# Stick-breaking attention of a four-layer trunk: one head at a time against head pairs by key blocks

## What is computed

```
def stick_breaking_block(q, k, v, q_pos, k_pos):
    z = jnp.einsum('bqhd,bkhd->bhqk', q, k) * (SB_HEAD_DIM ** -0.5)
    mask = k_pos[None, :] < q_pos[:, None]
    log_not = jnp.where(mask, jax.nn.log_sigmoid(-z), 0.0)
    rev = lax.cumsum(log_not, axis=3, reverse=True)
    tail = jnp.pad(rev[..., 1:], ((0, 0), (0, 0), (0, 0), (0, 1)))
    a = jnp.where(mask, jnp.exp(jax.nn.log_sigmoid(z) + tail), 0.0)
    return jnp.einsum('bhqk,bkhd->bqhd', a, v)
```

## Time and profile before

| what | value |
|---|---|
| median of 3 runs | 3169.05 us (3168.03 to 3176.56) |
| the profiled execution, first to last instruction | 3168.0 us |
| TensorE, VectorE, ScalarE, GpSimd busy | 2996.5, 1217.0, 877.9, 404.1 us |
| attention of one layer, first transpose to last values | 212.1 us |
| mean granted TensorE clock, whole span / between 225.1 and 396.6 us | 0.96 / 0.92 |

### The profile page before, as it was taken

The page is one execution under the profiler, slowest core; times in us unless marked ns, Lnnn a source line. Parts: engine busy times, 40 slices in busy tenths (PEclk is TensorE's granted clock), DMA queues, the critical chain, the costliest instruction groups (busy, mean ns, idle before and its releaser), DMA issues.

```text
span 3168.0 us, 49615 instructions
## 1 busy us (share of the span) xinstructions
PE 2996.5 (95%) x20839; PEld 2804.5 (89%) x20839; DVE 1217.0 (38%) x1596; ACT 877.9 (28%) x971; POOL 404.1 (13%) x557
## 2 busy tenths in 40 slices
PE   6999999999999599999998789999999899999998
PEld 6975599999999599999997679999999655999998
DVE  3332233333433543333346554333442322433433
ACT  2124432222311232222223233222321343322222
POOL 4023310000100500000103520000000232100001
PEclk8998999999999699999999889999999999999999
DMA  3230022222222122222221012222232200222221
GB/s 125 79 113 0 1 67 80 83 85 85 80 80 79 27 80 86 88 80 80 81 73 54 1 53 94 80 80 80 80 99 87 87 1 10 80 85 80 80 80 57
DMA packets 205443, 223.32 MB, mean 70 GB/s; under 512 B 3734, under 2 KB 200416, under 8 KB 205312
## 3 DMA queue, kind: packets, MB, share of 16 engines
q1 hardware_dynamic: 200336, 203.70, 20.1%
q0 software_dynamic: 4976, 17.74, 1.7%
HBM read 208.56 MB, written 12.86 MB: 70 GB/s over the span
## 4 chain that ended last, share of the span: by engine, by line
PE 77%; issue 16%; DVE 3%; POOL 2%; ACT 1%; DMA 1%; POOLq 0%; DVEq 0%; ACTq 0%
PE bank L308 62%; PE bank L407 5%; PE bank L429 3%; PE bank L392 3%; POOL big L1259 1%; PE bank L496 1%; PE bank L364 1%; DMA out<-mixs 1%; ACT big L688 0%; PE bank L541 0%; DVE mixs L971 0%; PE bank L538 0%; PE bank L550 0%; DVE stg L1064 0%; DVE stg L1091 0%
## 5 line engine op out<-in xcount | busy, mean ns | idle before, releaser
L308 PE MATMUL bank<-ahi,whi 128*128 128x288 f32 x3584 | 771.0, 297 | 6.5 <-DVE alo L875 6.5
L308 PE MATMUL bank<-alo,whi 128*128 128x288 f32 x3584 | 768.3, 296 | 0.0
L308 PE MATMUL bank<-ahi,wlo 128*128 128x288 f32 x3584 | 768.1, 296 | 0.0
L588 ACT ACTIVATE whi<-raw 128x2048 fp32r<-128x2048 f32 x191 | 364.6, 1909 | 900.0 <-PE bank L308 880.7
L308 PE MATMUL bank<-hhi,whi 128*128 128x288 f32 x2560 | 555.7, 299 | 52.6 <-DVE hlo L981 39.7
L308 PEld LDWEIGHTS bank<-ahi,whi 128*128 128x128 f32 x3584 | 579.2, 189 | 9.2 <-DVE wlo L850 6.6
L308 PEld LDWEIGHTS bank<-alo,whi 128*128 128x128 f32 x3584 | 578.7, 189 | 0.0
L308 PEld LDWEIGHTS bank<-ahi,wlo 128*128 128x128 f32 x3584 | 578.6, 189 | 0.0
L308 PE MATMUL bank<-hhi,wlo 128*128 128x288 f32 x2560 | 553.2, 298 | 0.0
L308 PE MATMUL bank<-hlo,whi 128*128 128x288 f32 x2560 | 553.0, 298 | 0.0
L850 DVE TENSOR_TENSOR wlo<-raw,whi 128x2048 fp32r<-128x2048 f32 x192 | 440.2, 2293 | 254.7 <-ACT whi L588 252.7
(11 more groups left out here) (232 smaller groups left out, 1952.7 us busy)
## 6 DMA issues: line engine op xcount, KB each, us to landing
raw<-in_mlp_w_up SPq DMA_DIRECT2D x64, 1024.0 KB, 5.4
raw<-in_mlp_w_down SPq DMA_DIRECT2D x64, 1024.0 KB, 5.0
raw<-in_sb_w_qkv SPq DMA_DIRECT2D x24, 1024.0 KB, 5.1
raw<-in_conv_w_in SPq DMA_DIRECT2D x12, 1024.0 KB, 5.2
raw<-in_gla_w_in SPq DMA_DIRECT2D x12, 1024.0 KB, 5.4
raw<-in_sb_w_o SPq DMA_DIRECT2D x8, 1024.0 KB, 5.0
out<-mixs POOLq DMA_DIRECT2D x3, 2048.0 KB, 13.2
out<-stg POOLq DMA_DIRECT2D x2, 2048.0 KB, 7.5
```

What stands on the lines that cost most here:

```text
L308: mm = pe.matmul(acc[h][:, 0:HALF], w[:, u, k, m * P:(m + 1) * P], a[:, k, h * HALF:(h + 1) * HALF], start=(k == 0 and w is whi and a is a ...
L588: act.activation(whi[:, 1 - u], raw[:, 1 - u], ACT.Copy).then_inc(w_hi, 1)
```

## The change

It rebuilds attention in layers 0 and 3 and moves what stands around it.

- **Units.** The loop runs over 24 units in place of 16 heads: a pair of heads by one of three key blocks (`WIDE` = 448, 512, 512 columns for each of the two heads), block 2 (the latest keys) first. The PSUM tensors become four `duo` tensors of two banks; a unit has one duo, even head in its first bank, odd head in its second, and three duos take turns.
- **Scores.** 1/8 is folded into Q by the projection's epilogue. The masks are added first (bf16), then each score matmul is issued for the even and the odd head one after the other.
- **Softplus.** ACT: exp and log over both heads at once. DVE: one instruction for clamp and maximum, then a copy into an fp32r high part and a subtraction into an fp32r low part (`parts(u)`, buffers shared with `whi`, `wlo`, `hlo`, `raw` and Q chunks).
- **Sums.** fp32r matmuls for both parts with a matrix of -1 in a triangle or everywhere (`sums`). Whole later blocks are added by matmuls over the parts of the units before, so POOL has no part in it. A part's buffer may be written again when `r_ready` has passed the last unit that reads it (`last_sum`).
- **Order.** PE: `scores(k + 2)`, `cumulative(k)`, `weighted_values(k - 1)`. ACT: `weights(k - 1)`, perhaps the output of a pair, `logs(k + 1)`, `exponents(k + 2)`. `scores(u)` waits for the weights of u - 3.
- **Transposes.** Cached K and V go through banks 6 and 7 between the first units (14 batches). The 10 batches of K follow the chunks of the output projection (`keys_out`), into the place of Q and into `e2`; their store comes after `add_squares` on POOL. DVE waits for all such stores before layer 1's and the last residual's epilogue, ACT for the V stores before the output projection.
- **Projections.** Everywhere, chunks now take turns over banks 0 to 3 alone: a chunk waits for the epilogue of the chunk two before. SP loads the second slab of the attention's output weights only when `r_ready` has reached 21 of 24 units.

The diff's core:

```diff
-                        acc = bank[4 * u + 2 * m:4 * u + 2 * m + 2]
-                        pe.wait_ge(acc_free, 2 * (base + s) + m + 1)
+                        acc = bank[2 * m:2 * m + 2]
+                        pe.wait_ge(acc_free, 2 * (base + s) + m + 3)
...
+                def scores(u):
+                    p, b, z = u // 3, 2 - u % 3, zduo[u % 3]
+                    if u >= 3:
+                        pe.wait_ge(a_ready, first + u - 2)
...
+                    def scored(lo, hi, keys, q_lo):
+                        for e in range(2):
+                            r = slice(HD * e, HD * e + HD)
+                            k = keys(r)
+                            mm = pe.matmul(z[0:k.shape[1], e, lo:hi], k, big[r, p, q_lo:q_lo + hi - lo], start=False,
+                                           stop=False, skip_group_check=True)
...
+                    if b == 2:
+                        scored(0, 256, lambda r: big[r, 8 + p, 256:384], 256)
+                        scored(256, 384, lambda r: big[r, 8 + p, 384:512], 384)
+                        scored(384, 448, lambda r: big[r, 8 + p, 512:576], 512).then_inc(z_ready, 1)
+                    elif b == 1:
+                        scored(0, 384, lambda r: big[r, 8 + p, 128:256], 128)
+                        scored(384, 448, lambda r: CKT[r, p, 0:128], 512)
+                        scored(448, 512, lambda r: CKT[r, p, 128:256], 512).then_inc(z_ready, 1)
+                    else:
+                        scored(0, 512, lambda r: big[r, 8 + p, 0:128], 0).then_inc(z_ready, 1)
...
+                    for part, ready in ((0, sp_hi), (1, sp_lo)):
+                        pe.wait_ge(ready, first + u + 1)
+                        for e in range(2):
+                            def acc(which, lo, hi, back, of):
+                                return pe.matmul(z[:, e, lo:hi], sums[:, which, :], parts(u - back)[part][:, e, of:of + hi - lo],
+                                                 start=False, stop=False, skip_group_check=True)
+                            mm = acc(0, 0, WIDE[u % 3], 0, 0)
+                            if b == 2:
+                                mm = acc(1, 128, 256, 0, 256)
+                            elif b == 1:
+                                acc(1, 128, 384, 1, 0)
+                                acc(1, 256, 384, 1, 256)
+                                acc(1, 384, 448, 1, 384)
+                                acc(1, 448, 512, 1, 384)
+                                mm = acc(1, 384, 448, 0, 448)
+                            elif b == 0:
+                                acc(1, 128, 512, 1, 0)
+                                acc(1, 256, 512, 2, 0)
+                                mm = acc(1, 384, 512, 2, 256)
...
+                    def valued(o, lo, hi, v, rows, of, start, stop):
+                        for e in range(2):
+                            hc = slice((2 * p + e) * HD, (2 * p + e + 1) * HD)
+                            mm = pe.matmul(o[HD * e:HD * e + HD, lo:hi], v(hc), a[0:rows, e, of:of + hi - lo], start=start,
+                                           stop=stop, skip_group_check=True)
...
+                for k in range(1, UNITS):
+                    if k + 2 < UNITS:
+                        scores(k + 2)
+                    cumulative(k)
+                    weighted_values(k - 1)
+                weighted_values(UNITS - 1)
...
+                    dve.wait_ge(l_ready, first + u + 1)
+                    dve.scalar_tensor_tensor(s, s, LN_MAX, zduo[u % 3][:, :, 0:w], ALU.min, ALU.max).then_inc(sp_ready, 1)
+                    dve.wait_ge(sp_ready, first + u + 1)
+                    if u >= 4:
+                        dve.wait_ge(r_ready, first + last_sum(u - 4) + 1)
+                    dve.tensor_copy(hi, s).then_inc(sp_hi, 1)
+                    dve.wait_ge(sp_hi, first + u + 1)
+                    dve.tensor_tensor(lo, s, hi.bitcast(F32), ALU.subtract).then_inc(sp_lo, 1)
...
+                for k in range(2, UNITS + 1):
+                    weights(k - 1)
+                    if k % 3 == 1:
+                        output((k - 4) // 3)
+                    if k + 1 < UNITS:
+                        logs(k + 1)
+                    if k + 2 < UNITS:
+                        exponents(k + 2)
```

More of the change, by code:

```diff
@@ L317, in body @@
                             aside(s, True)
-                slabs(pe, count, body, peel(count, norm, False))
+                        if between is not None:
+                            between(s, m)
+                slabs(pe, count, body, peel(count, norm, between is not None))
             def sum_squares(i):
@@ L588, in split_next, with run @@
                 act.activation(whi[:, 1 - u], raw[:, 1 - u], ACT.Copy).then_inc(w_hi, 1)
-            def run(base, count, epilogue, norm=None, last=False, beside=None):
+            def run(base, count, epilogue, norm=None, last=False, beside=None, between=None):
+                whole = last or between is not None
                 def body(s, u):
@@ L598, in body @@
                             epilogue(s, m)
+                            if between is not None:
+                                between(s, m)
                         if beside is not None:
                             beside(s)
-                for s in range(peel(count, norm, last)):
+                for s in range(peel(count, norm, whole)):
                     body(s, s % 2)
-                if peel(count, norm, last) < count:
-                    first = peel(count, norm, last)
+                if peel(count, norm, whole) < count:
+                    first = peel(count, norm, whole)
                     with act.Fori(0, (count - first) // 2) as i:
@@ L705, in stick_breaking, with cached_keys @@
-                output(HEADS // 2 - 1)
+                def cached_keys(n):
+                    sb_evacuate(sb_index, n, CKT[:, 2 * n:2 * n + 2, :].rearrange("p c k -> p (c k)"), bank[7][:, :])
+                exponents(0)
+                cached_keys(1)
+                logs(0)
+                exponents(1)
+                cached_keys(3)
+                logs(1)
+                values(sb_index, 5)
+                exponents(2)
+                values(sb_index, 7)
+                weights(0)
@@ new lines, in stick_breaking @@
+                values(sb_index, 9)
+                logs(2)
+                values(sb_index, 11)
+                values(sb_index, 13)
+                exponents(3)
+                for k in range(2, UNITS + 1):
[6 more added lines that the diff above has]
+                        exponents(k + 2)
+                output(PAIRS - 1)
@@ L850, in split, with run @@
                 dve.tensor_tensor(wlo[:, u], raw[:, u], whi[:, u].bitcast(F32), ALU.subtract).then_inc(w_lo, 1)
-            def run(base, count, epilogue, norm=None, last=False, beside=None):
+            def run(base, count, epilogue, norm=None, last=False, beside=None, between=None, unrolled=False):
                 def body(s, u):
@@ L860, in body @@
                         epilogue(s, u, m)
+                        if between is not None:
+                            between(s, m)
                     if beside is not None:
                         beside(s)
-                slabs(dve, count, body, peel(count, norm, last))
+                slabs(dve, count, body, peel(count, norm, last or unrolled or between is not None))
             def at(t, j):
```

417 lines of the change are left out of this document (225 added, 192 removed).

## The result

The changed kernel took 3018.53 us (median, 3017.96 to 3019.27), the kernel before 3172.81 us on the same chip (3168.03 to 3177.65). The ratio is 0.952, with a 95% interval from 0.950 to 0.954. The profiled execution of after has a span of 3016.9 us, that of before 3168.0: 151.1 us went. The prediction was 3040 in a range from 3000 to 3115. The time is inside the range, but the forecast gain of 129 us was 22 us too small, and the time lies between the forecast and rival C (3003).

What follows compares the result with a forecast made beforehand. TensorE, busy 95% of the span, was taken as the bound. Attention's 212.1 us a layer would become 142.1, 147 with clock loss; two layers gain 130, less 1, giving 3040 us, range 3000 to 3115.

Steps and rivals of the forecast that it cites:

- rival C: Scores and values of two heads wholly side by side, no clock loss: 14.0 us a pair, 3003 us in all; chance 0.07.
- Part 1, sums: Sums as fp32r matmuls on TensorE: 6.84 us a pair, where two heads' sums with masks took 9.28.
- Part 2, scores and values: Scores and values issued by pairs of heads, partly overlapping on TensorE: 8.1 us a pair, between 11.66 and 5.83.
- A1 A2 B1 B2: Assumed issue order of two heads' records, two each: a lone 512-column pair takes 3 slots for 4, factor 0.69.
- wholly-side-by-side end: Lower bound for a pair's scores and values if both heads overlap entirely on TensorE: 5.83 us.
- sign against overlap: Earlier trace at 209.84, two 64-column records before the next head: nothing was hidden, read as speaking a little against overlap.
- Pace: A pair of heads in the attention loop: 6.84 + 0.74 + 8.1 = 15.7 us, against 22.7 before; serial 19.2.
- The clock: Clock loss in attention: half of the earlier kernel's 7.9% on 120 us, 5 us a layer.
- Part 3, before the loop: Transposes in 14 batches between the first units: loop starts at 16.6 us overlapped, 17.4 serial.
- K transposes: Ten batches moved behind the first output projection chunks: 10 x 0.46 = 4.6 us on TensorE, still paid.
- The bare weights pass: At the end of the attention loop one ACT weights pass is uncovered: 1.2 us a layer.
- Part 4, accumulators: Two projection accumulators instead of four: tight at each norm, 0 to 0.3 us, eight times, 1 us taken.

Runs made afterwards that it cites:

- experiment 5: The changed kernel with weighted_values(k - 1) issued before cumulative(k) in the loop; 3081.51 us, ratio to the kernel before 0.971.
- experiment 6: The changed kernel with two more VectorE instructions of 512 elements a unit from unit 4 on, results unused; 3021.74 us, ratio to before 0.952.
- experiment 1: The changed kernel with masks and scores of the even head first, then those of the odd head; 3083.64 us, ratio to before 0.971.
- experiment 2: The changed kernel with value matmuls of the even head first, then those of the odd head; 3042.46 us, ratio to before 0.957.
- experiment 3: The changed kernel with sums as plain fp32 matmuls over one part, the low part left out; 3075.72 us, ratio to before 0.968.
- experiment 7: The changed kernel without the ten K transposes behind the output projection, their evacuations and the K stores; 3012.17 us.
- experiment 8: The changed kernel with ScalarE's wait for the convolution's four small stores moved behind the next slab's weight copy; 3012.5 us, ratio to before 0.949.

## Why the prediction was right or wrong

**The direction and the bound** were right in the main: what changed TensorE's own time changed the pace. But ACT's weights pass did become last, by 0.13 and 0.17 us in two of three units. The prediction had said so for the case of whole overlap (values of 0.97 us, 0.2 us a unit coming back as a wait), and put it into C alone. Experiments 5 and 6 show which cover mattered: ACT's pass behind the sums, not DVE.

**Part 1, sums.** Forecast 6.84 us a pair, measured 7.38. The 0.54 too little are 9 us over 16 pairs. Block by block 1.40, 3.29 and 2.69 stand against 1.26, 3.04 and 2.54. No run shows the forecast's prices of an fp32r matmul (0.227 us for 512 columns, 0.200 for 448, 0.173 for 384, 0.120 for 256, 0.10 for 64); they were the author's estimate. Its 0.114 us for 128 is that of a transpose, 4.58 / 40. The timeline of the changed kernel shows in their place:

```profile
287.49 0.50 PE L446 MATMUL bank<-whi,sums 128*128 128x512 f32 x1
287.83 0.53 PE L446 MATMUL bank<-split_r,sums 128*128 128x256 f32 x4
...
293.42 0.68 PE L446 MATMUL bank<-whi,sums 128*128 128x512 f32 x2
293.94 0.34 PE L446 MATMUL bank<-split_r,sums 128*128 128x256 f32 x2
294.11 0.62 PE L446 MATMUL bank<-whi,sums 128*128 128x512 f32 x2
```

A 512-column matmul at the start of a group took 287.83 - 287.49 = 0.34 us, one of 512 with one of 384 took 0.52 (forecast 0.40), and one of 256 with one of 128 only 0.17 (forecast 0.234). So the short ones were cheap and the long ones cost more than their estimate.

**Part 2, scores and values: the step that was mis-sized.** Forecast 8.1 us a pair, measured 3.41 + 3.46 = 6.87; 1.2 a pair, 20 us over the run. I assumed the order A1 A2 B1 B2, with three slots for four records. The array runs A1 B1, A2 B2, two slots; experiments 1 and 2 show that the second head is free. The wholly-side-by-side end, 5.83, wasn't met either: 0.30 of the 6.87 are the waits for ACT, and the rest is of the size of the 0.1 us at each end of a group of one form. The forecast's 9.81 us for 5888 fp32 columns agrees with the 0.43 us between the records of a 512-column matmul, two records each: 1.68 ns a column. Its 0.033 us a record, on which the 1.85 rests, is an estimate that no run shows; what the runs showed is about 0.1 us at each end of a group of one form, and the new kernel has shorter groups and more of them. Nor does a run show the 0.48 + 0.26 us that the forecast took for a pair's eight masks: they took 0.8. The error in the scores and values (20 us too much) and that in the sums (9 too little) partly cancel, which is luck. I had read the earlier trace rows as a sign against overlap and gave whole overlap 0.07; two records of 64 columns at a change of the tile form were no test of it. Whole overlap had deserved about as much as the forecast.

**Pace.** 15.06 measured for 15.7: 7.38 + 0.8 + 6.87. C's mechanism (whole overlap, no clock loss, a short wait for ACT) is what came, at C's price of 14.0 plus 1 us a pair. The forecast came near by its number more than by its mechanism.

**The clock.** I charged 5 us a layer, half of before's loss (171.50 us for fourteen heads, where 14 x 11.35 are 158.9: 7.9%); the loop ran at 1.00 and lost nothing: 10 us of the 22. Why before's ran at 0.92 isn't settled. Idle time of TensorE alone isn't it: in experiment 5 it was busy for 91.57 of 110 us of the loop, less than before's 94%, and had 0.98. Fp32 sums alone aren't it either: experiment 3's loop had 1.00. Nor are lone heads alone: with lone values the loop had 1.00 (experiment 2), and with lone scores too, after a stretch at half clock ahead of it (experiment 1). No run has the old order and types together without the rest of the old kernel.

**Part 3, before the loop.** Forecast 16.6, measured 16.40. K transposes: forecast 4.6, measured 4.3 (experiment 7). The bare weights pass of 1.2 us at the end isn't bare: values of the unit before the last lie over all but some 0.15 us of it, the same cover that I had counted in the loop.

```profile
323.10 2.26 PE L477 MATMUL bank<-big,mixs 128*64 128x384 f32 x16
```

These are the last two units' values: the last unit's begin 1.18 us after those before, which take 1.02 without a wait (experiment 5).

**Part 4, accumulators.** Forecast 0 to 0.3 us at each of eight norms, 1 us. At the norms it was nothing, and a norm wasn't the tight place. The tight place is where DVE waits for a store with a weight split ahead of an epilogue, after the convolution: once, 0.5 us, since TensorE goes on after one chunk's epilogue (0.82 us) instead of after the split ahead of it.

**The sum.** A layer was forecast at 147.1 (142.1 and the clock) and took 16.4 + 114.9 + 4.3 = 135.6. The 11.5 are: eight pairs 5.1, clock 5.0, the bare pass 1.2, prologue and K transposes 0.5, less 0.3 for scores and sums done before the loop. Two layers make 23, where the span shows 22.

## What to carry to other kernels

When two matmuls on disjoint halves of the array can stand next to each other in the queue, with nothing of the same half in between, take it as likely that the second is free, as both forms showed here, and look at what one alone costs, not at half of both. Before pricing an overlap from a place where it seems to fail, see whether that place has enough columns to show it. And when a step is sped up, find the pass of another engine that is covered by its neighbour (here 1.03 us of ACT under 1.0 to 1.1 of values): the order of two lines was worth 63 us.

## What the runs showed of the hardware

- Two fp32 matmuls on disjoint row halves, or into disjoint column halves, ran wholly side by side, weight loads included: 1.06 us for four records of 512 columns, and 1.05 us for the two of one head (experiment 1); 1.06 us for the values of two heads in block 2, and 2.10 one head after the other (experiment 2). A lone matmul on half of the array was thus no cheaper than a pair.
- A group of matmuls of one tile form costs more at its ends. A 512-column fp32 matmul between groups of other forms took 1.05 us; inside a group its second record takes 0.43. Splitting the groups adds two more changes of tile form a unit, and masks grew by about 0.1 us for it, 0.23 + 0.16 (experiment 1) against 0.28. By these rows an end of a group costs about 0.1 us here. That the change of form is the cause, and not another property of a new group, is not shown apart.
- The store of the conv state took 17.1 us before, 17.7 after and 20.9 us in experiment 8, for the same bytes. Why they differ is open.
- The loop's granted clock was 0.92 before, 1.00 after and 0.98 in experiment 5; experiment 1 had half the clock for 17.1 us at the start of attention, and 1.00 from there on.
